# Two weight chunks ahead of each layer norm by token tiles, a weight rounding behind the norm, an offset from a tensor and a scalar

## The chip, the cores and the metric

The kernel runs on one core of one Trainium2 chip. The metric is the device time of one execution in microseconds (us); the median of three runs before the change is 1275.93 us (1275.86 to 1277.51).

## What is computed

Two blocks of two layers each on 256 tokens of width 1024, in fp32. The first block (attention of three kinds and squared-ReLU MLPs, RMS norms) isn't touched. In the second block each layer has a mixer and a gated feed-forward part, and after each of them a residual and a layer norm:

```python
for layer in range(DEPTH):                      # DEPTH = 2
    y = even_mixer(x, ...) if layer % 2 == 0 else odd_mixer(x, ...)
    x = layer_norm(ALPHA * x + y, ln1_g[layer], ln1_b[layer])
    f = conv_ffn(x, ffn_w_up[layer], ...)       # 1024 -> 2 x 2816, conv, silu(gate) * val, 2816 -> 1024
    x = layer_norm(ALPHA * x + f, ln2_g[layer], ln2_b[layer])

def layer_norm(x, g, b):
    mu = x.mean(-1, keepdims=True)
    var = jnp.square(x - mu).mean(-1, keepdims=True)
    return (x - mu) * lax.rsqrt(var + LN_EPS) * g + b
```

The kernel numbers these four layer norms 5 (after the even mixer), 6 (after the first feed-forward part), 7 (after the odd mixer) and 8 (the last one, whose result is the output).

## The kernel before, in words

**Weights as a stream.** All weights come as 186 chunks of 1 MB (128 partitions x 2048 fp32) in one fixed order. To keep fp32 precision, each chunk is split in two: ScalarE rounds it into `w_hi` (`cut`, L1090), GpSimd subtracts and rounds the rest into `w_lo` (L2350, four instructions of 512 columns a chunk). TensorE multiplies in three products (`three`, L284 to L286: hi by hi, hi by lo, lo by hi), or in two instructions in `dense_beside` (L332, L334). There are 3 buffers for the raw chunk and 4 for the split one. SyncE loads raw chunk c when `w_lo` of chunk c-3 is made. `cut(c)` waits for that load and for TensorE's last use of chunk c-4 (`chunk_used`), and TensorE waits for `w_lo_ready` of a chunk before it uses it.

**The order by hand.** No scheduler orders the work: each engine has its own program, written out line by line, and runs in order. ScalarE's `cut` of a chunk therefore stands at a fixed place between its other work, three chunks ahead (`AHEAD = 3`) of the step beside which it is written. `chunks_and_root` (L1101) issues the cuts that belong to the last chunks ahead of a norm and then loads the table of the square root.

**The work ahead of a norm.** There are two token tiles, t = 0 and t = 1, of 128 tokens each, and two output halves of 512 columns. Ahead of norms 5 and 7, `last_half` works through the last two chunks of the mixer's output projection (`ev_out`, `od_out`): chunk 2 with both token tiles side by side, step by step as its four inputs come in, then (for norm 7 after `sums`, which makes the root mean square of the gated heads) chunk 3, first all of t = 0, then all of t = 1. Ahead of norms 6 and 8, `down_by_tokens` works through 11 chunks with both token tiles side by side, except the last chunk, which is done for t = 0 first.

**The norm.** `norm` of VectorE has a `piece(n, t)` for each half and token tile: the residual is added (L1670, L1672 or L1674), statistics are taken (L1681), and with the second half the mean and variance (L1683). ScalarE makes the square root (L1175), VectorE's `invert(t)` the reciprocal (L1688) and the offset -mean x inverse (L1689, `scalar_tensor_tensor` on 128x1), and ScalarE normalises with them (L1188; L1182 in norm 8). VectorE works through its pieces in the order (0,0), (0,1), (1,0), then `invert(0)`, (1,1), `invert(1)`. TensorE turns the normalised tiles from tokens by features to features by tokens (`turned`, L401, 16 transposes), VectorE and ScalarE apply gain and bias and split the result into `xs_hi` and `xs_lo` (L1600), and TensorE goes on with the next stage: `fup0` after norm 5, `dt` and `od_xbc` after norm 6, `fup1` after norm 7. After norm 8 the result is stored in four transfers.

**Behind a norm.** ScalarE's first work behind norms 5 and 7 is the cut of fup chunk 3, then in `gated` one cut an iteration. Behind norm 6 it is the cut of `od_xbc` chunk 2, then Abs, Exp and Ln of the step sizes (L1507 to L1509), Exp (L1510), and per `od_xbc` chunk one cut, two activations (L1516) and a Silu (L1519), with VectorE's taps (L2253) in between.

Of the kernel before, what the change touches and what calls it, by code (L numbers as in the profile page):

```python
# [18 lines left out]
ALU = mybir.AluOpType  # L19
# [4 lines left out]
TT = T // P  # L24
# [9 lines left out]
AHEAD = 3  # L34
# [10 lines left out]
START, _n = {}, 0  # L45
# [27 lines left out]
def build(nc, x, stream, params, consts, onehot, logc, relb, evb_row, ln_rows, pool_w, pool_mat, vec_row, vec_scratch, out):  # L73
    with ExitStack() as ctx:
# [5 lines left out]
        def S(name):  # L80
            if name not in sems:
                sems[name] = ctx.enter_context(nc.semaphore(name))
            return sems[name]
# [27 lines left out]
        with hidden:  # L111
            hT_hi = hidden.enter_context(nc.sbuf_tensor("hT_hi", [P, 32, T], F32R))
            hT_lo = hidden.enter_context(nc.sbuf_tensor("hT_lo", [P, 32, T], F32R))
# [59 lines left out]
        sums = bank[7]  # L173
        r_bc, eps_s, r_col = rstd[:, :], mu[:, :], small[:, 60:62]

        deviation, inverse, offset, inv_y = (stats[:, 24 + 2 * n:26 + 2 * n] for n in range(4))
        moments = [stats[:, 32 + 2 * t:34 + 2 * t] for t in range(TT)]
# [34 lines left out]
        XS, n = {}, 0  # L212
# [5 lines left out]
        HT, n = {}, 0  # L218
# [10 lines left out]
        def claim(pe, key):  # L229

            while turn[0] % 8 >= rotating[0]:
                turn[0] += 1
            b = turn[0] % 8
            turn[0] += 1
            return claim_bank(pe, key, b)
# [11 lines left out]
        def filled(ins, key):  # L247
            b = made[key][0]
            fcount[b] += 1
            ins.then_inc(S(f"bank{b}_filled"), 1)  # L250
            made[key][2:] = [f"bank{b}_filled", fcount[b]]

        def filled_by_chunk(key, c):
            made[key][2:] = ["chunk_used", c + 1]
# [18 lines left out]
        def _(pe):  # L273
# [6 lines left out]
            def used_up(ins):  # L280
                ins.then_inc(S("chunk_used"), 1)
# [57 lines left out]
            def half_views(c):  # L339
                return (x.rearrange("p a b -> p (a b)").rearrange("p (k n) -> p k n", k=4) for x in chunk(c))  # L340
# [16 lines left out]
            def by_tokens(o, hi, lo, kw, src, k, t, start, stop):  # L357

                s = slice(t * P, (t + 1) * P)
                return three(o[:, :], src[0][:, k, s], src[1][:, k, s], hi[:, kw, :], lo[:, kw, :], start=start, stop=stop)  # L360

            def last_half(name, i, src, wait, sums=lambda: None):

                c = START[name] + 2
                hi, lo = half_views(c)
                o = [claim(pe, (name, 1, t)) for t in range(TT)]
                for k in range(4):
                    pe.wait_ge(S("xs_ready"), XS[wait] - 3 + k)
                    for t in range(TT):
                        last = by_tokens(o[t], hi, lo, k, src, k, t, start=(k == 0), stop=(k == 3))  # L370
                used_up(last)
                for t in range(TT):
                    filled_by_chunk((name, 1, t), c)
                sums()
                hi, lo = half_views(c + 1)
                for t in range(TT):
                    o = claim(pe, (name, 1, 2 + t))
                    for k in range(4):
                        last = by_tokens(o, hi, lo, k, src, k, t, start=(k == 0), stop=(k == 3))
                    if t == 0:  # L380
                        filled(last, (name, 1, 2))
                used_up(last)
                filled_by_chunk((name, 1, 3), c + 1)
                turned(i)
# [20 lines left out]
            def down_by_tokens(name, kt, ready, i):  # L405

                chunks, o = 2 * kt // 4, {}
                for c in range(chunks):
                    hi, lo = half_views(START[name] + c)
                    steps = [(u, t) for u in range(4) for t in range(TT)] if c < chunks - 1 else \  # L410
                        [(u, t) for t in range(TT) for u in range(4)]
                    for u, t in steps:
                        n, k = divmod(4 * c + u, kt)
                        key = (name, 2 * n + t)
                        if n == 0 and t == 0:
                            pe.wait_ge(S("hidden_ready"), ready + k + 1)
                        if k == 0:
                            o[n, t] = claim(pe, key)
                        last = by_tokens(o[n, t], hi, lo, u, (hT_hi, hT_lo), k, t, start=(k == 0), stop=(k == kt - 1))
                        if k == kt - 1 and (n, t) != (1, 1):  # L420
                            filled(last, key)
                    used_up(last)
                filled_by_chunk((name, 3), START[name] + chunks - 1)
                if i < 8:
                    turned(i)
# [86 lines left out]
            hi, lo = chunk(START["va"])  # L512
            o = claim(pe, "va")
            for t in range(TT):
                for k in range(8):
                    s = slice(t * P, (t + 1) * P)
                    last = three(o[:, t * P:(t + 1) * P], xs_hi[:, k, s], xs_lo[:, k, s], hi[:, k, 0:P], lo[:, k, 0:P],
                                 start=(k == 0), stop=(k == 7))
# [5 lines left out]
            o = claim(pe, "qa_sums")  # L524
            for t in range(TT):
                for n in range(4):
                    last = mm(o[:, 4 * n + t:4 * n + t + 3:2], sq[:, n, t * P:(t + 1) * P], cc("blk", 128)[:, 0:128:64],
                              start=True, stop=True)
# [544 lines left out]
        def _(act):  # L1073
# [26 lines left out]

            def chunks_and_root(name, total, first=0):  # L1101

                for c in range(first, total):
                    cut(START[name] + c + AHEAD)
                warm(ACT.Sqrt)

# [63 lines left out]
            def norm(i):  # L1170

                g, b, p0 = ln_par(i)
                for t in range(TT):
                    act.wait_ge(S("variance"), 2 * (i - 5) + t + 1)
                    af(deviation[:, t:t + 1], moments[t][:, 1:2], ACT.Sqrt, bias=pc("eps_ln")).then_inc(S("deviated"), 1)  # L1175
                    if i == 8 and t == 1:
                        return
                    act.wait_ge(S("inverted"), 2 * (i - 5) + t + 1)
                    factor = dict(bias=offset[:, t:t + 1], scale=inverse[:, t:t + 1])
                    if i == 8:  # L1180
                        key = last_piece(i, 0, t)
                        drained(af(token_half(0, t), by_tile(bank[made[key][0]][:, :]), ACT.Identity, **factor), key)  # L1182
                        continue
                    key = last_piece(i, 1, t)
                    o = bank[made[key][0]]
                    for n in PAIRS if t == 0 else (0, 1):
                        src = token_pair(n, t) if n < 2 else by_tile(o[:, (n - 2) * T:(n - 1) * T])
                        ins = af(token_pair(n, t), src, ACT.Identity, **factor)  # L1188
                        if n == 3:
                            drained(ins, key)  # L1190
                        else:
                            ins.then_inc(S("normed_act"), 1)

                def affine(n):
                    o = full(act, ("turn", i, n))
                    for j in range(2):
                        k = 2 * n + j
                        af(o[:, j * T:(j + 1) * T], o[:, j * T:(j + 1) * T], ACT.Identity, bias=pc(b, p0 + k),
                           scale=pc(g, p0 + k)).then_inc(S("affine_act"), 1)

                def high(n):
                    if n < 2:
                        act.wait_ge(S("affine_dve"), 2 * (i - 5) + n + 1)
                    else:
                        act.wait_ge(S("affine_act"), 4 * (i - 5) + 2 * n - 2)
                    o = bank[made[("turn", i, n)][0]]
                    af(xs_hi[:, 2 * n:2 * n + 2, :], o[:, :].rearrange("p (a b) -> p a b", a=2), ACT.Copy).then_inc(S("xs_hi"), 1)

                affine(2)
                high(0)  # L1210
                high(2)
                high(1)
                affine(3)
                high(3)

            def mlp(name, opened=False):
                hb = HT[name]
# [366 lines left out]
        def _(dve):  # L1584
# [75 lines left out]
            def norm(i, factor=None):  # L1660
# [24 lines left out]
                def invert(t):  # L1685

                    dve.wait_ge(S("deviated"), 2 * (i - 5) + t + 1)
                    link(v.reciprocal(inverse[:, t:t + 1], deviation[:, t:t + 1]))  # L1688
                    v.scalar_tensor_tensor(offset[:, t:t + 1], moments[t][:, 0:1], -1.0, inverse[:, t:t + 1], ALU.mult, ALU.mult)\  # L1689
                        .then_inc(S("inverted"), 1)  # L1690

                def gained(n, t):
# [8 lines left out]
                        .then_inc(S("result_dve"), 1)  # L1701

                piece(0, 0)
                piece(0, 1)
                piece(1, 0)
                if i == 8:
                    dve.wait_ge(S("ln_rows_loaded"), 16 * 4)
# [10 lines left out]
                    finished(0, 1)  # L1718
                    return
                invert(0)  # L1720
                piece(1, 1)
                invert(1)
                key = last_piece(i, 1, 1)
# [891 lines left out]
```

## Time and profile before

| | |
|---|---|
| median of three runs | 1275.93 us |
| the profiled execution, its own time | 1281.55 us |
| its span (first to last instruction) | 1279.7 us |
| TensorE busy | 1211.6 us (95%) |
| GpSimd busy | 955.8 us (75%) |
| ScalarE busy | 679.5 us (53%) |
| VectorE busy | 623.2 us (49%) |
| mean granted TensorE clock | 0.971 |

PE is TensorE, DVE is VectorE, ACT is ScalarE, POOL is GpSimd. A row of a timeline has the start in us from the span's start, the duration in us, the engine, the line, the operation, what it writes and reads, the shape, and in brackets the idle time just before it and who ended it. All instructions of the same kind that follow each other are merged into one row (x2, x4).

### The profile page before, as it was taken

What the parts mean: (1) busy time and instruction counts of PE and PEld (TensorE: products, weight loads), DVE (VectorE), ACT (ScalarE), POOL (GpSimd) and SP (SyncE); (2) the same over time, 40 slices, a digit from 0 to 9 for tenths busy, and PEclk for the clock granted to TensorE, in tenths of its full rate; (3) what the DMA queues carried; (4) which work ended last, traced back from release to release, by engine and by line L of the source; (5) the groups of instructions that cost most, each with busy time, mean ns of one, the idle gap of its engine ahead of it and who ended that gap; (6) DMA issues with size and microseconds to landing.
All of it is one profiled execution on the core that took longest, in us unless ns stands there. A gap on an engine that the chain in (4) does not pass through costs nothing.

```text
span 1279.7 us, 20261 instructions
## 1 busy us (share of the span) xinstructions
PE 1211.6 (95%) x7822; PEld 1081.0 (84%) x7822; DVE 623.2 (49%) x1076; ACT 679.5 (53%) x920; POOL 955.8 (75%) x750
## 2 busy tenths in 40 slices
PE   4899999999989999999999998999997898999997
PEld 4788998999968998999988777888886876888885
DVE  4866344210485244210542755777405646587712
ACT  5365655444565655444454346656546565656741
POOL 4846679978843779979795446899895854789985
PEclk9799999999999999999999898999998989999999
DMA  6562345554431446545553123555554442436551
GB/s 262 191 184 104 133 155 208 197 178 176 174 124 43 165 145 217 195 168 178 196 193 134 66 74 133 189 206 203 184 201 156 139 159 102 165 138 234 204 184 64
DMA packets 33132, 208.56 MB, mean 163 GB/s; under 512 B 3432, under 2 KB 7656, under 8 KB 8472
## 3 DMA queue, kind: packets, MB, share of 16 engines
q1 hardware_dynamic: 29728, 199.22, 43.6%
q10 hardware_dynamic: 3320, 8.14, 2.0%
q8 instruction: 62, 1.02, 0.3%
q14 instruction: 22, 0.18, 0.0%
HBM read 206.29 MB, written 1.59 MB: 162 GB/s over the span
## 4 chain that ended last, share of the span: by engine, by line
POOL 56%; issue 24%; PE 16%; DVE 2%; ACT 1%; DMA 0%; POOLq 0%; DVEq 0%; SPq 0%; ACTq 0%
POOL w_lo L2350 56%; PE bank L332 6%; PE bank L334 3%; PE bank L284 2%; PE bank L286 2%; PE bank L285 2%; ACT w_hi L1090 0%; DMA raw<-stream 0%; DVE stats L1681 0%; PE bank L1032 0%; ACT arena L1528 0%; ACT h L1188 0%; DVE bank L1695 0%; POOLq L2347 0%; PE bank L1047 0%
## 5 line engine op out<-in xcount | busy, mean ns | idle before, releaser
L2350 POOL TENSOR_TENSOR w_lo<-raw,w_hi 128x512 fp32r<-128x512 f32 x744 | 953.1, 1319 | 308.1 <-ACT w_hi L1090 307.9
L1090 ACT ACTIVATE w_hi<-raw 128x2048 fp32r<-128x2048 f32 x186 | 353.8, 1910 | 187.5 <-PE bank L286 110.0
L332 PE MATMUL bank<-xs,w_hi 128*128 128x512 f32 x1024 | 361.7, 398 | 3.1 <-DVE xs L1600 3.1
L334 PE MATMUL bank<-xs,w_lo 128*128 128x256 f32 x1024 | 287.3, 281 | 0.0
L332 PEld LDWEIGHTS bank<-xs,w_hi 128*128 128x128 f32 x1024 | 193.6, 189 | 50.4 <-issue 3.9
L284 PE MATMUL bank<-xs,w_hi 128*128 128x256 f32 x624 | 183.3, 294 | 20.6 <-POOL w_lo L2350 17.6
L284 PE MATMUL bank<-hT_hi,w_hi 128*128 128x256 f32 x680 | 194.7, 286 | 2.1 <-issue 1.9
L334 PEld LDWEIGHTS bank<-xs,w_lo 128*128 128x128 f32 x1024 | 194.5, 190 | 0.0
L286 PE MATMUL bank<-hT_hi,w_lo 128*128 128x256 f32 x680 | 192.4, 283 | 0.0
L285 PE MATMUL bank<-xs,w_hi 128*128 128x256 f32 x624 | 179.8, 288 | 0.0
L286 PE MATMUL bank<-xs,w_lo 128*128 128x256 f32 x624 | 179.4, 288 | 0.0
L284 PEld LDWEIGHTS bank<-xs,w_hi 128*128 128x128 f32 x624 | 122.8, 197 | 27.0 <-issue 26.2
L285 PE MATMUL bank<-hT_lo,w_hi 128*128 128x256 f32 x512 | 145.0, 283 | 0.0
L284 PEld LDWEIGHTS bank<-hT_hi,w_hi 128*128 128x128 f32 x680 | 128.6, 189 | 5.4 <-issue 5.2
L286 PEld LDWEIGHTS bank<-hT_hi,w_lo 128*128 128x128 f32 x680 | 128.6, 189 | 0.0
L285 PEld LDWEIGHTS bank<-xs,w_hi 128*128 128x128 f32 x624 | 123.0, 197 | 0.4 <-issue 0.2
L286 PEld LDWEIGHTS bank<-xs,w_lo 128*128 128x128 f32 x624 | 122.9, 197 | 0.0
L1762 DVE TENSOR_REDUCE tb<-bank 128x256 f32<-128x512 f32 x128 | 82.2, 684 | 63.9 <-PE bank L334 63.8
L1816 DVE SCALAR_TENSOR_TENSOR bank<-tb,par,bank 128x254 f32<-128x254 f32 (+1 forms) x176 | 85.8, 488 | 40.4 <-ACT bank L1253 35.7
L285 PEld LDWEIGHTS bank<-hT_lo,w_hi 128*128 128x128 f32 x512 | 96.6, 189 | 0.0
L284 PE MATMUL bank<-w_hi,hT_hi 128*128 128x512 f32 x212 | 84.3, 398 | 2.2 <-DVEq L2322 2.2
L285 PE MATMUL bank<-w_lo,hT_hi 128*128 128x512 f32 x212 | 83.7, 395 | 0.0
(318 smaller groups left out, 1600.5 us busy)
## 6 DMA issues: line engine op xcount, KB each, us to landing
raw<-stream SPq DMA_DIRECT2D x186, 1024.0 KB, 4.8
arena<-ln_rows ACTq DMA_DIRECT2D x4, 1024.0 KB, 4.9
arena<-vec_scratch ACTq DMA_DIRECT2D x8, 256.0 KB, 9.0
con<-consts SPq DMA_DIRECT2D x1, 1288.0 KB
h<-x SPq DMA_DIRECT2D x1, 1024.0 KB, 5.0
out<-h SPq DMA_DIRECT2D x4, 256.0 KB, 2.3
con<-pool_mat ACTq DMA_DIRECT2D x1, 768.0 KB, 8.1
vec_scratch<-vec_row ACTq DMA_DIRECT2D x1, 512.0 KB
```

The lines of the kernel that those rows point to most:

```text
L284: mm(out, lh, rh, start=start, stop=False, skip_group_check=True)
L285: mm(out, lh, rl, start=False, stop=False, skip_group_check=True)
L286: return mm(out, ll, rh, start=False, stop=stop, skip_group_check=True)
L332: mm(o[j][:, :], hi[:, k, s], xs[:, k, :, :].rearrange("p a t -> p (a t)"), start=(k == tiles_in[0]), stop=False, skip_group_check=True)
L334: last = mm(o[j][:, 0:T], lo[:, k, s], xs_hi[:, k, :], start=False, stop=(k == tiles_in[-1]), skip_group_check=True)
L1090: af(w_hi[:, c % CUT].rearrange("p a b -> p (a b)"), raw[:, c % RAW, :], ACT.Copy)\
L1762: ins = v.tensor_reduce(tb[:, i % 2, j * T:(j + 1) * T], o[:, :].rearrange("p (a t) -> p t a", a=2), AX.X, ALU.add)
L1816: ins = v.scalar_tensor_tensor(t[:, j, tap:T], u[:, j, 0:T - tap], pc("fcw", 132 * layer + 44 * (2 - tap) + ti), t[:, j, tap:T], ALU.mult, ...
L2350: ins = nc.gpsimd.tensor_tensor(w_lo[:, slot_c].rearrange("p a b -> p (a b)")[:, part], raw[:, slot_r, part], w_hi[:, slot_c].rearrange("p ...
```

## The change

It does four things. (1) `last_half` now ends chunk 2 of t = 0 first, goes through chunk 3 of t = 0, and then does what is left of chunk 2 and all of chunk 3 for t = 1. (2) `down_by_tokens` does its last two chunks, not the last one alone, for t = 0 first and then for t = 1. (3) The last cut ahead of norms 5, 6 and 7 (chunk 2 of `fup0`, chunk 1 of `od_xbc`, chunk 2 of `fup1`) moves behind ScalarE's part of the norm. (4) The offset is made by `tensor_scalar` from the mean, the inverse (a scalar for each partition) and -1.0; and in norms 5 and 7 `piece(0, 1)` moves behind `invert(0)`.

```diff
@@ last_half
-                for k in range(4):
-                    pe.wait_ge(S("xs_ready"), XS[wait] - 3 + k)
-                    for t in range(TT):
-                        last = by_tokens(o[t], hi, lo, k, src, k, t, start=(k == 0), stop=(k == 3))
-                used_up(last)
+                steps = [(0, 0), (0, 1), (1, 0), (1, 1), (2, 0), (3, 0)]
+                for k, t in steps:
+                    if t == 0:
+                        pe.wait_ge(S("xs_ready"), XS[wait] - 3 + k)
+                    last = by_tokens(o[t], hi, lo, k, src, k, t, start=(k == 0), stop=(k == 3))
+                filled(last, (name, 1, 0))
+                sums()
+                hi2, lo2 = half_views(c + 1)
                 for t in range(TT):
-                    filled_by_chunk((name, 1, t), c)
-                sums()
-                hi, lo = half_views(c + 1)
-                for t in range(TT):
-                    o = claim(pe, (name, 1, 2 + t))
+                    if t == 1:
+                        for k in (2, 3):
+                            last = by_tokens(o[1], hi, lo, k, src, k, 1, start=False, stop=(k == 3))
+                        used_up(last)
+                        filled_by_chunk((name, 1, 1), c)
+                    o2 = claim(pe, (name, 1, 2 + t))
                     for k in range(4):
-                        last = by_tokens(o, hi, lo, k, src, k, t, start=(k == 0), stop=(k == 3))
+                        last = by_tokens(o2, hi2, lo2, k, src, k, t, start=(k == 0), stop=(k == 3))
@@ down_by_tokens (step(c, hi, lo, u, t) is the body of the old inner loop)
+                for c in range(chunks - 2):
                     hi, lo = half_views(START[name] + c)
+                    for u in range(4):
+                        for t in range(TT):
+                            last = step(c, hi, lo, u, t)
                     used_up(last)
+                final = {c: tuple(half_views(START[name] + c)) for c in (chunks - 2, chunks - 1)}
+                for t in range(TT):
+                    for c in final:
+                        hi, lo = final[c]
+                        for u in range(4):
+                            last = step(c, hi, lo, u, t)
+                        if t == 1:
+                            used_up(last)
@@ chunks_and_root
-                for c in range(first, total):
+                for c in range(first, total - 1):
@@ norm of ScalarE, at its end
                 affine(3)
                 high(3)
+                cut(START[{5: "fup0", 6: "dt", 7: "fup1"}[i]] - 1 + AHEAD)
@@ invert of VectorE
-                    v.scalar_tensor_tensor(offset[:, t:t + 1], moments[t][:, 0:1], -1.0, inverse[:, t:t + 1], ALU.mult, ALU.mult)\
+                    v.tensor_scalar(offset[:, t:t + 1], moments[t][:, 0:1], inverse[:, t:t + 1], -1.0, ALU.mult, ALU.mult)\
                         .then_inc(S("inverted"), 1)
@@ norm of VectorE
                 piece(0, 0)
-                piece(0, 1)
+                if i in (6, 8):
+                    piece(0, 1)
                 piece(1, 0)
...
                 invert(0)
+                if i in (5, 7):
+                    piece(0, 1)
                 piece(1, 1)
                 invert(1)
```

## Rows read from the trace of the kernel before

**Rows 1.** The page: TensorE's busy time, and the chain that ended last, by engine.
```profile
PE 1211.6 (95%) x7822; PEld 1081.0 (84%) x7822; DVE 623.2 (49%) x1076; ACT 679.5 (53%) x920; POOL 955.8 (75%) x750
...
POOL 56%; issue 24%; PE 16%; DVE 2%; ACT 1%; DMA 0%; POOLq 0%; DVEq 0%; SPq 0%; ACTq 0%
```

**Rows 2.** Busy time by stretch: stretch, us, busy of each engine, clock, DMA share, GB/s.
```profile
775.70:783.00 7.30, 3.62 (x18) 2.40 (x17) 5.94 (x14) 5.67 (x13) 1.67 (x2) 0.76 0.46 177
783.00:786.40 3.40, 3.40 (x11) 2.92 (x12) 1.94 (x3) 2.51 (x5) 0.00 (x0) 0.51 0.00 0
...
968.10:979.40 11.30, 3.92 (x17) 2.77 (x17) 9.91 (x14) 5.66 (x13) 4.45 (x4) 0.70 0.52 186
...
1087.20:1090.10 2.90, 2.90 (x9) 2.51 (x10) 1.95 (x3) 2.05 (x5) 0.00 (x0) 0.50 0.02 6
```

**Rows 3.** Timeline of VectorE in norm 6.
```profile
965.47 0.70 DVE L1674 SCALAR_TENSOR_TENSOR bank<-h,bank 128x512 f32<-128x512 f32 x1 [25.08 <-PE bank L286]
...
968.00 4.57 DVE L1689 SCALAR_TENSOR_TENSOR stats<-stats 128x1 f32<-128x1 f32 x1
972.49 0.68 DVE L1674 SCALAR_TENSOR_TENSOR bank<-h,bank 128x512 f32<-128x512 f32 x1
```

**Rows 4.** Timeline of GpSimd around norm 6.
```profile
953.85 18.70 POOL L2350 TENSOR_TENSOR w_lo<-raw,w_hi 128x512 fp32r<-128x512 f32 x15
982.90 5.04 POOL L2350 TENSOR_TENSOR w_lo<-raw,w_hi 128x512 fp32r<-128x512 f32 x4 [10.35 <-ACT w_hi L1090]
```

**Rows 5.** Timeline of TensorE ahead of norm 5: 21 matmuls lie between the two starts.
```profile
770.57 0.39 PE L286 MATMUL bank<-w_hi,hT_hi 128*128 128x512 f32 x1
...
775.33 0.39 PE L286 MATMUL bank<-w_hi,hT_hi 128*128 128x512 f32 x1
```

**Rows 6.** Timeline of ScalarE behind norm 6.
```profile
980.92 1.91 ACT L1090 ACTIVATE w_hi<-raw 128x2048 fp32r<-128x2048 f32 x1
983.32 0.42 ACT L1507 ACTIVATE arena<-arena 8x256 f32<-8x256 f32 x1 [0.50 <-DVE arena L2239]
```

**Rows 7.** Timeline of VectorE in norm 5.
```profile
776.09 0.69 DVE L1672 TENSOR_TENSOR bank<-bank,h 128x512 f32<-128x512 f32 x1
...
778.42 0.16 DVE L1688 RECIPROCAL stats<-stats 128x1 f32<-128x1 f32 x1 [0.67 <-ACT stats L1175]
```

**Rows 8.** Timelines of VectorE in norm 7, and of TensorE's gated sums ahead of it.
```profile
1069.29 0.48 DVE L2302 SCALAR_TENSOR_TENSOR xs<-bank,par,xs 128x256 fp32r<-128x256 f32 x1 [0.56 <-ACT xs L1540]
...
1073.76 0.75 DVE L1670 SCALAR_TENSOR_TENSOR h<-bank,stats,h 128x512 f32<-128x512 f32 x1
...
1080.27 0.75 DVE L1670 SCALAR_TENSOR_TENSOR bank<-bank,stats,h 128x512 f32<-128x512 f32 x1
...
1082.61 0.17 DVE L1688 RECIPROCAL stats<-stats 128x1 f32<-128x1 f32 x1 [0.61 <-ACT stats L1175]
...
1071.31 1.84 PE L1063 MATMUL bank<-con,arena 128*128 128x1 f32 x16
```

**Rows 9.** Timelines of VectorE in norm 8, and of GpSimd's last roundings.
```profile
1268.30 0.70 DVE L1674 SCALAR_TENSOR_TENSOR bank<-h,bank 128x512 f32<-128x512 f32 x1 [25.06 <-PE bank L286]
...
1271.81 0.68 DVE L1674 SCALAR_TENSOR_TENSOR bank<-h,bank 128x512 f32<-128x512 f32 x1
...
1249.12 12.53 POOL L2350 TENSOR_TENSOR w_lo<-raw,w_hi 128x512 fp32r<-128x512 f32 x10
```

**Rows 10.** Behind norm 5: TensorE's line L332 (22 chunks), GpSimd's next rounding, VectorE's first fold.
```profile
L332 PE MATMUL bank<-xs,w_hi x352: 391/395/764, 783.0 to 907.7; 128*128 128x512 f32 x176
...
787.46 5.05 POOL L2350 TENSOR_TENSOR w_lo<-raw,w_hi 128x512 fp32r<-128x512 f32 x4 [10.08 <-ACT w_hi L1090]
...
790.36 1.29 DVE L1762 TENSOR_REDUCE tb<-bank 128x256 f32<-128x512 f32 x2 [5.03 <-PE bank L334]
```

**Rows 11.** Other VectorE instructions with operands in SBUF: line L2061, line L2242.
```profile
L2061 DVE TENSOR_SCALAR arena<-arena,par x1: 1425/1425/1425, 623.4 to 623.4; 12x256 f32<-12x256 f32 x1
...
L2242 DVE SCALAR_TENSOR_TENSOR arena<-arena x1: 831/831/831, 987.4 to 987.4; 8x256 f32<-8x256 f32 x1
```

More of the change, by code:

```diff
@@ L407, in down_by_tokens, with step @@
                 chunks, o = 2 * kt // 4, {}
-                for c in range(chunks):
-                    hi, lo = half_views(START[name] + c)
[L410 to L421, printed above, removed]
-                    used_up(last)
+                def step(c, hi, lo, u, t):
+                    n, k = divmod(4 * c + u, kt)
+                    key = (name, 2 * n + t)
+                    if n == 0 and t == 0:
+                        pe.wait_ge(S("hidden_ready"), ready + k + 1)
+                    if k == 0:
+                        o[n, t] = claim(pe, key)
+                    last = by_tokens(o[n, t], hi, lo, u, (hT_hi, hT_lo), k, t, start=(k == 0), stop=(k == kt - 1))
+                    if k == kt - 1 and (n, t) != (1, 1):
+                        filled(last, key)
+                    return last
+                for c in range(chunks - 2):
+                    hi, lo = half_views(START[name] + c)
+                    for u in range(4):
+                        for t in range(TT):
+                            last = step(c, hi, lo, u, t)
+                    used_up(last)
+                final = {c: tuple(half_views(START[name] + c)) for c in (chunks - 2, chunks - 1)}
[6 more added lines that the diff above has]
+                            used_up(last)
                 filled_by_chunk((name, 3), START[name] + chunks - 1)
```

## The prediction

> **What bounds the kernel.** I began with the page: TensorE is busy 95% of the span, yet most of the chain that ended last is GpSimd's rounding [rows 1]. A chunk costs GpSimd some 5.05 us and TensorE 5.67 us (22 chunks in the 124.7 us between the first and last start of L332) [rows 10]. So in a dense stage TensorE sets the pace and the rounding follows closely: moving a rounding costs nothing only while a stock of finished chunks lasts. The stretches at the norms then show where TensorE stands: 7.3 us in norm 5 and 11.3 us in norm 6, with under 4 us of work in each [rows 2]. There the chain is VectorE, ScalarE, transposes, VectorE. In VectorE's timeline of norm 6 one row stands out: the offset, a single column, takes 4.57 us [rows 3]. It ends when GpSimd's continuous run ends, 953.85 + 18.70 = 972.55 [rows 4]. Piece (1,1), whose matmuls had long ended (968.1), starts only after it, at 972.49.
>
> **A first look at the pace.** One fp32 matmul of 512 columns takes (775.33 - 770.57) / 21 = 0.227 us [rows 5]; a unit of three 0.68, one token tile of a chunk (12) 2.72, a whole chunk 5.44 us. The change neither adds nor removes a matmul.
>
> **Norm 6.** Token tile 0 now ends one half chunk earlier: its last piece starts at 965.47 - 2.72 = 962.75 [rows 3]. Up to the offset it takes 968.00 - 965.47 = 2.53 us, so the offset is issued at 965.3. GpSimd still rounds the chunk before until some 967.7 (972.55 less one chunk of 5.0) [rows 4]. The price of the new instruction has bounds: 0.16 us if it doesn't need what GpSimd holds, or a wait to 967.7, 2.4 us, if it does. `tensor_scalar` with both sides in SBUF has taken 1.43 us where GpSimd ran [rows 11], so I take the wait. It costs nothing here: TensorE is busy with tile 1 until 968.1, and ScalarE's four normalisations (some 0.5 us each, 2.0) end at 969.7, when the variance of tile 1 is due (968.15 + 1.65, the 2.53 less root and reciprocal, = 969.8). The cover is TensorE's own work on tile 1. Piece (1,1) starts at 968.15 instead of 972.49: 4.34 us. The root of tile 1 no longer queues behind those normalisations; the same wait in norm 5 was 0.67 us, and 0.36 without a queue: another 0.3. TensorE would restart at 979.4 - 4.65 = 974.75.
>
> That isn't yet the gain, since the moved cut now stands on ScalarE's queue. ScalarE's part of the norm ended at 980.92; now at 976.3. Then come two cuts of 1.91 us, to 980.1, and then Abs, which had started at 983.32 [rows 6]. The earlier limit, the end of `dt` and one VectorE step of 0.5 us, lies at 978.6 and isn't last any more. So what follows moves by 3.2 us, not 4.65. In `od_xbc` the loop of cut, activations and taps on ScalarE and VectorE is slower than TensorE and sets the pace, so 3.2 us is what goes on. The chunk whose rounding moved is ready at 978.2 + 5.05 = 983.3; TensorE needs it after `dt` (3.4 us) and `od_xbc` chunk 0 (48 matmuls of 0.12, 5.8 us), at 974.75 + 9.2 = 983.9 at the earliest. It is close, but TensorE doesn't set the pace there. **-3.2 us** (bounds -2.2, if TensorE restarts at half rate for all of `dt`, and -4.65).
>
> **Norm 5.** Chunk 2 of tile 0 ends two units (1.36 us) earlier. VectorE then takes (0,0), waits for tile 0's second half (30 units of 0.227 after 764.9: 771.7), inverts at 773.7 to 774.1, and does (0,1) until 775.5. TensorE ends at 775.7, so (1,1) starts at 775.8 instead of 776.09: 0.3 us; the root without a queue gives 0.3 [rows 7]. Here TensorE restarts at half rate: 0.51 granted (1.2 GHz) from 783.0 to 786.4, behind a norm in which it mostly stood [rows 2]. If full rate comes back at the same moment, only half of a start 0.6 us earlier remains: **-0.3 us** (bounds 0 and -0.6).
>
> The moved cut costs nothing as long as the stock holds. The first cut behind the norm started 1.9 us ahead of its rounding at 787.46 [rows 10]; 0.6 us earlier the moved one takes its place, 784.9 to 786.8, its rounding until 791.8, the next one until 796.9. TensorE needs them at 790.36 + 5.6 = 796.0 and 801.6 [rows 10], some 4 us later each, and GpSimd gains 0.6 us a chunk. In ScalarE's queue both cuts end at 788.7, ahead of the first fold at 790.36 that it waits for. The raw loads behind it, three chunks on, land 6 us before their cuts. Norm 7's stock is alike.
>
> **Norm 7.** The last input is ready at 1069.77. Ahead of the sums TensorE then has one unit left instead of two, and these start at 1070.5 instead of 1071.31: 0.8 us [rows 8]. But TensorE, which used to fill the wait for that input with tile 1, stands about 0.7 us, and ends at 1079.2 instead of 1078.6. VectorE: (0,0) at 1072.9, (1,0) at 1075.0 when its bank is full, offset by 1077.5, (0,1) until 1079.0, (1,1) at 1079.25 instead of 1080.27 [rows 8]: 1.0 us, and 0.25 for the root (0.61 against 0.36). Half rate again (0.50) from 1087.2 to 1090.1 [rows 2]: **-0.6 us** (bounds -0.3 and -1.3).
>
> **Norm 8.** Tile 0's chain moves from 1268.30 to 1265.6 and is out of the way; (1,1) starts when TensorE ends, 1270.97, instead of 1271.81 [rows 9]. The rest is unchanged: **-0.8 us**.
>
> **Edits without a price.** The offset as `tensor_scalar` changes nothing by itself once no rounding runs beside it (norms 5, 7, 8) or it is hidden (6). Semaphores, transfers and bytes stay as they are; SyncE's load for the moved chunk has landed long before.
>
> **Sum.** -0.3 - 3.2 - 0.6 - 0.8 = -4.9 us, against the profiled execution: 1281.55 to 1276.6. That execution lies 5.6 us above the median of the runs; taken from the median, 1275.93 - 4.9 = 1271.0.
>
> **A rule against the trace.** The offset outlasted four GpSimd instructions of some 1.25 us [rows 3, 4]. The Trainium skill (SBUF — State Buffer, "Who interferes with whom") says that whoever issues first gets the shared port pair "for the whole instruction", and the other blocks; by that alone one waits for one instruction, at most 1.3 us, and norm 6 would have had 3.3 us less to give. The row shows more than three times that. The same section says that `tensor_scalar` can enter a mode that takes the pair too; L2061 agrees.
>
> **Rivals.**
> *A. The 4.57 us belong to the profiled execution.* The 5.6 us between it and the median are suspiciously like it. If the offset gets through at the first end of a GpSimd instruction (968.9), piece (1,1) started at 969.0 in the timed runs, norm 6 gives 1.1 us at the restart, and the second cut takes that back at Abs (980.1 against 979.8). What remains is -0.3 - 0.6 - 0.8 + 0.3 = -1.4: **1274.5**. For it: in most rows like L2242 the wait is under 1.3 us. Against it: the program is the same in each run, and GpSimd ran without a pause. 0.22.
> *B. A half-rate stretch of TensorE more or less.* Such a stretch costs about 1.7 us (half of 3.4) [rows 2]. One less: -6.6, **1269.3**, 0.12; it would show in the clock of the restarts.
> *C. A lockout behind norm 6.* After the change GpSimd rounds three chunks back to back there, 978.3 to 993.4. L2242, with both inputs in SBUF, is issued at 984.2; it took 0.83 us where GpSimd's chunk had just ended [rows 11]. If it is held as the offset was, until GpSimd pauses at 993.4, the taps start at 994.8 instead of 988.4, and `od_xbc` is 6.4 us late: -4.9 + 6.4 = +1.5, **1277.4**. It decides once the wait passes the 2.2 us that VectorE has there. With A it would be about 1281. 0.07.
> *D. The change doesn't get tile 0 earlier,* because TensorE waits for `w_lo` of the last chunk, which it now needs 2.72 us sooner. At norm 8 the rounding ends at 1261.65 [rows 9] and is needed at 1262.8 (1268.2 less two token tiles of a chunk), so only if GpSimd slips by over 1.1 us; norms 6 and 8 then give half, 2.0 us less: **1273.0**, 0.04.
>
> **Numbers.** The forecast, 1271.0, has 0.55. Its bounds, -3.3 and -7.3, give 1268.6 to 1272.6; A asks for 1274.5 and some tenths, so 1268.3 to 1275.2 leaves out C and the tails. About 0.2% (2.6 us) can be told from no change: faster is the forecast, B and most of D, 0.73; same is A and most of C, 0.22; slower 0.05.
>
> **What would show it.** The offset of norm 6's tile 1 at 0.16 us; piece (1,1) within 0.1 us of TensorE's last matmul in all four norms; TensorE's stretch without main matmuls in norm 6 near 6.7 us instead of 11.3; two cuts back to back behind each of norms 5 to 7, and Abs right behind them; no wait for `w_lo` in fup chunks 2 to 5. I am wrong if Abs moves by the full 4.6 us, if L2242 takes over 2 us, or if the profile gains 5 us and the timed runs don't.

## The result, and the profile after

The changed kernel took 1269.65 us (median of 5 runs, 1267.99 to 1270.86) against 1275.93 for the one before (5 runs): ratio 0.9947, interval 0.9921 to 0.9972, so 6.3 us less. The forecast was 1271.0 us. The profiled execution took 1269.36 us with a span (first to last instruction) of 1267.6, 12.1 us under the span of before. That is more than the timed gain, so the first question is where the two traces part. One execution of the kernel before in the last group below took 4124.69 us; it is in no comparison.

The page of the changed kernel; beside it belong [rows 1]:
```profile
PE 1205.4 (95%) x7822; PEld 1076.6 (85%) x7822; DVE 609.6 (48%) x1076; ACT 679.1 (54%) x920; POOL 957.2 (76%) x750
...
POOL 71%; issue 27%; PE 1%; POOLq 0%; DVE 0%; DVEq 0%
```
Every engine has as many instructions as before. The largest difference is VectorE's: it is busy 13.6 us less (623.2 to 609.6), and 12.4 us of that was waiting inside two instructions, shown below; TensorE is busy 6.2 us less.

To place the time I cut every trace where TensorE gives a weight chunk free. There are 186 such releases, in the same order in all kernels. A norm's stretch is the last two chunks ahead of it and what follows until the first chunk behind it is released (for norm 6 that chunk is `dt`). "mixer" lies between the stretches of norms 6 and 7; "end" is the last two chunks and all behind them; "start" is what comes before norm 5's stretch. "sum" is the three norms and the end, "+ mixer" the same with the mixer, and the last columns are the last two chunks ahead of norms 6 and 8 alone. From the semaphore updates in the traces, in us:
```
kernel           start   norm5  norm6  mixer  norm7  end    sum     + mixer  6 / 8
before           764.85  25.49  25.57  80.92  30.63  19.71  101.40  182.32   10.88 / 10.88
before_again     753.88  25.48  25.58  81.00  30.69  19.70  101.45  182.45   10.88 / 10.88
after            755.12  25.29  22.46  81.15  30.01  19.69   97.45  178.62   11.67 / 11.66
after_again      753.25  25.12  23.56  81.09  30.02  19.73   98.43  179.51   12.86 / 11.71
offset_only      754.15  24.79  22.67  81.87  27.83  19.81   95.10  176.96   10.88 / 10.88
cut_only         765.29  24.65  22.07  81.71  29.38  19.71   95.81  177.53   10.88 / 10.88
offset_and_cut   756.13  24.79  22.14  81.47  29.42  19.81   96.16  177.63   10.88 / 10.88
tokens_only      753.21  28.68  25.28  81.43  32.99  19.21  106.16  187.61   11.69 / 11.25
after_stt        754.61  24.96  23.48  81.32  32.34  19.26  100.04  181.36   12.86 / 11.29
lazy             764.80  25.14  22.64  80.48  32.24  18.90   98.92  179.40   10.88 / 10.88
down_tiles       753.16  24.82  22.04  81.19  29.48  18.90   95.24  176.43   10.88 / 10.88
before_norope    761.12  25.10  28.72  80.36  32.08  19.71  105.61  185.97   10.88 / 10.88
after_norope     761.47  24.97  24.64  80.43  32.26  19.31  101.18  181.60   12.89 / 11.29
```
Of the 12.1 us, 9.7 lie in the start, in code that the change does not touch; 3.95 lie in the norms and the end; the other stages took about 1.5 us longer (the stretch of `fup1` alone 1.2).

Windows of the changed kernel at the norms, columns as in [rows 2]:
```profile
766.00:772.60 6.60, 2.44 (x17) 1.71 (x16) 5.73 (x13) 4.55 (x11) 0.00 (x0) 0.84 0.06 24
773.00:777.30 4.30, 4.30 (x15) 3.72 (x14) 1.37 (x2) 4.27 (x4) 1.50 (x2) 0.50 0.00 0
959.00:965.30 6.30, 2.03 (x17) 1.51 (x15) 5.51 (x13) 3.84 (x9) 0.00 (x0) 0.98 0.42 164
...
1073.00:1077.60 4.60, 4.57 (x14) 3.92 (x15) 1.99 (x3) 4.57 (x6) 1.13 (x1) 0.50 0.01 4
```
Norm 6 is the third line: 6.3 us where [rows 2] had 11.3, and GpSimd is not busy in it at all (0.00; 4.45 before). Behind norms 5 and 7 TensorE still restarts at a granted clock of 0.50.

Behind norm 6 the restart is different from before. `dt`, before and now:
```profile
979.40:982.80 3.40, 3.38 (x26) 3.18 (x27) 1.96 (x3) 3.37 (x5) 0.00 (x0) 1.00 0.00 0
```
```profile
965.30:969.80 4.50, 4.50 (x26) 4.50 (x27) 1.93 (x3) 4.47 (x6) 1.08 (x1) 0.65 0.00 0
```
The same matmuls took 4.5 us at a granted clock of 0.65 where they had taken 3.4 at 1.00: 1.1 us of the earlier restart was lost again at once. before_again took 3.4 us as well; in all other profiles below `dt` took 4.4 to 5.5.

VectorE's timeline in norm 6:
```profile
955.67 0.17 DVE L1706 RECIPROCAL stats<-stats 128x1 f32<-128x1 f32 x1 [0.36 <-ACT stats L1192]
955.87 0.21 DVE L1707 TENSOR_SCALAR stats<-stats 128x1 f32<-128x1 f32 x1
959.01 0.70 DVE L1692 SCALAR_TENSOR_TENSOR bank<-h,bank 128x512 f32<-128x512 f32 x1 [2.93 <-PE bank L286]
...
961.05 0.17 DVE L1706 RECIPROCAL stats<-stats 128x1 f32<-128x1 f32 x1 [0.36 <-ACT stats L1192]
961.25 0.21 DVE L1707 TENSOR_SCALAR stats<-stats 128x1 f32<-128x1 f32 x1
...
974.39 0.91 DVE L2263 SCALAR_TENSOR_TENSOR arena<-arena 8x256 f32<-8x256 f32 x1 [3.84 <-ACT arena L1527]
```
The 4.57 us of [rows 3] are gone. Piece (1,1), at 959.01, now waits for TensorE; in all four norms it starts within 0.1 us of the end of TensorE's last chunk. The last line (L2242 in the kernel before) is rival C's candidate: 0.91 us.

GpSimd's timeline around norm 6:
```profile
938.91 18.78 POOL L2371 TENSOR_TENSOR w_lo<-raw,w_hi 128x512 fp32r<-128x512 f32 x15
968.72 21.80 POOL L2371 TENSOR_TENSOR w_lo<-raw,w_hi 128x512 fp32r<-128x512 f32 x16 [11.03 <-ACT w_hi L1107]
```
The first run lasts until 957.69, so tile 0's offset (955.87) was issued beside it and still took 0.21 us.

ScalarE's timeline behind norm 6:
```profile
966.74 3.71 ACT L1107 ACTIVATE w_hi<-raw 128x2048 fp32r<-128x2048 f32 x2
970.34 0.40 ACT L1525 ACTIVATE arena<-arena 8x256 f32<-8x256 f32 x1
```
Two cuts back to back and Abs right behind, as forecast. `dt` ends at 969.78, so the other limit, `dt` and one VectorE step of 0.5 us, lies at the same place.

TensorE's waits between 947 and 953 us:
```profile
PE bank L284 <- POOL w_lo L2371: 0.5, 1, 0.5
```
This one was not forecast. It lies ahead of norm 6, and there is one like it ahead of norm 8: the last two chunks took 10.88 us before and 11.67 and 11.66 now.

### The profile page after: what moved, and what is told of

It reads as the page before. It is cut to its first block, busy times and chain, and to the rows that moved or that the text cites. A ratio compares the mean times of both kernels' runs of the same rounds, so it can differ in the third digit from the quotient of the medians.

```text
span 1267.6 us, 20263 instructions
## 1 busy us (share of the span) xinstructions
PE 1205.4 (95%) x7822; PEld 1076.6 (85%) x7822; DVE 609.6 (48%) x1076; ACT 679.1 (54%) x920; POOL 957.2 (76%) x750
## 4 chain that ended last, share of the span: by engine, by line
POOL 71%; issue 27%; PE 1%; POOLq 0%; DVE 0%; DVEq 0%
POOL w_lo L2371 71%; PE bank L284 0%; PE bank L286 0%; PE bank L285 0%; POOLq L2368 0%; DVE bank L1713 0%; POOLq L2377 0%; DVE stats L1699 0%; DVE bank L1692 0%; DVEq L74 0%; DVE h L1718 0%; DVE stats L1701 0%; DVE stats L1707 0%; POOLq L2371 0%; DVE stats L1706 0%
## 5 line engine op out<-in xcount | busy, mean ns | idle before, releaser
L332 PE MATMUL bank<-xs,w_hi 128*128 128x512 f32 x1024 | 364.3, 401 | 3.9 <-DVE xs L1618 3.8
L332 PEld LDWEIGHTS bank<-xs,w_hi 128*128 128x128 f32 x1024 | 194.4, 190 | 52.4 <-issue 4.4
```

The source lines that it names most:

```text
L332: mm(o[j][:, :], hi[:, k, s], xs[:, k, :, :].rearrange("p a t -> p (a t)"), start=(k == tiles_in[0]), stop=False, skip_group_check=True)
```

## The experiments

Kernels of one group ran on the same chip and share the runs of the kernel before: first the repeats and the pair without one multiplication; then the single parts with after_stt; then lazy, offset_and_cut and down_tiles. The medians of the kernel before in the three groups are 1274.56, 1275.99 and 1275.17 us, and each ratio is against its own group.

**Both kernels again, unchanged.** Edit: none.

> The kernel before, once more, against itself. Theory 1 (lockouts by chance): the profile of before lost 9.1 us in one VectorE multiplication in the first 50 us (two SBUF inputs, held while GpSimd rounded two chunks), which the profile of after did not (1.04 us there), in code that the change doesn't touch. Then the profile of this run may show any length from 0.7 to 9 us for it, while the offset of norm 6 may be 4.6 us or less; the timed runs lie between 1272 and 1278. Rival: the lockouts are the same in each execution of one program; then this profile shows 9.1 us and 4.57 us again, within 0.1 us.

> The changed kernel, once more. Theory 1: ratio 0.995 +- 0.003, and the early multiplication (L1880) may be long here too in some executions (single times near 1277 would show it). Rival: it is 1.04 us again, and all times are within 1268 to 1271.

Measured: before_again 1274.51 us, ratio 1.0007 (0.9991 to 1.0022); after_again 1269.98, ratio 0.9967 (0.9954 to 0.9981), 4.6 us under the 1274.56 of before on that chip. The runs of before_again fall into two bands, six at 1271.6 to 1272.8 and six at 1276.2 to 1278.6. None of after_again is near 1277; they lie between 1266.8 and 1273.4.

VectorE's line of the offset in before_again (duration min/median/max in ns):
```profile
L1689 DVE SCALAR_TENSOR_TENSOR stats<-stats x8: 159/160/4747, 764.6 to 1265.7; 128x1 f32<-128x1 f32 x8
```
The norm 6 wait came again, 4.75 us: it does not belong to one execution, and rival A falls. In norms 5 and 7 the other long ones took 0.61 and 1.26. But before_again's start was 11.0 us shorter than before's. VectorE and GpSimd at the first rope pass, in the kernel before:
```profile
39.14 9.10 DVE L1859 TENSOR_TENSOR arena<-arena 128x512 f32<-128x512 f32 x1
...
29.03 18.66 POOL L2350 TENSOR_TENSOR w_lo<-raw,w_hi 128x512 fp32r<-128x512 f32 x15
```
And in the changed kernel:
```profile
39.46 1.04 DVE L1880 TENSOR_TENSOR arena<-arena 128x512 f32<-128x512 f32 x1
...
29.92 29.24 POOL L2371 TENSOR_TENSOR w_lo<-raw,w_hi 128x512 fp32r<-128x512 f32 x22
```
The same instruction, untouched by the change, took 9.10 us once and 1.04 once, with GpSimd rounding beside it both times (0.78 in before_again, 0.79 in after_again). This is most of what the two profiles differ by beyond the norms, and no part of the gain. It is not tied to the old kernel: the profiled executions of cut_only and lazy had it too and took 1279.25 and 1281.44 us, 11 and 12 above their medians. A median of 6 to 12 runs may hold any share of such executions, so read the stretches beside the ratios.

**The multiplication that was held, left out of both kernels.**
```diff
-                link(v.tensor_tensor(pair_of(n), pair_of(n), over(c, 2), ALU.mult))
```

> The kernel before without the multiplication of the queries and keys by the cosine in VectorE's rotation of the first block (L1859, left out in all three calls; its output is another). Theory 1: what is gained is the mean lockout, some 3 to 6 us: 1270 to 1273. If the timed runs don't have the lockout: 1 to 2 us for the instructions themselves, 1274 to 1275.

> The changed kernel with the same multiplication left out. Against the kernel before with it left out, this is the change alone: by the profiles -0.2 (norm 5), -3.1 (norm 6), -0.6 (norm 7), -0.75 (end), +0.8 (TensorE waits 0.5 us twice for w_lo of the last chunk ahead of norms 6 and 8, since both chunks are waited for at the start), and 0 or +1.2 for TensorE's pitch in fup1: -2.7 to -3.9. If the timed 6.3 us belong to the change, it is 1263 to 1267 and the difference stays over 5.

Measured: 1283.07 us, ratio 1.0068 (1.0046 to 1.0089), and 1278.33, ratio 1.0026 (1.0012 to 1.0040). Both got slower with less to do, against the expectation. VectorE's next instruction with two inputs in SBUF, in before_norope:
```profile
L1873 DVE TENSOR_TENSOR arena<-arena x1: 12570/12570/12570, 45.6 to 45.6; 128x512 f32<-128x512 f32 x1
```
In after_norope the same one took 12.53. The wait moved to the next candidate and grew by a third, so as a way to remove it the experiment failed. As a comparison it serves: with the wait alike in both, the pair differs by 4.7 us in the medians (2.7 to 3.9 had been expected, and over 5 if all of the first 6.3 were the change's) and by 4.4 in the stretches. The old offset of norm 6 was held again, 5.04 us.

**The offset alone, in the kernel before.**
```diff
-  v.scalar_tensor_tensor(offset[:, t:t + 1], moments[t][:, 0:1], -1.0, inverse[:, t:t + 1], ALU.mult, ALU.mult)
+  v.tensor_scalar(offset[:, t:t + 1], moments[t][:, 0:1], inverse[:, t:t + 1], -1.0, ALU.mult, ALU.mult)
```

> The kernel before with the offset by tensor_scalar alone. In the profile of after that instruction took 0.21 us while GpSimd rounded. Theory 1 (it doesn't take what GpSimd holds; the lockout of the offset is most of what norm 6 gave): 0.2 us for all eight, VectorE's piece (1,1) of norm 6 starts at once when TensorE ends, 4.3 us earlier, and since one cut alone stands ahead of Abs, 3.5 to 4.6 us of it go on; in norm 7 the 1.26 us become 0.2, worth 0.5 to 1: together -4 to -5.5 us, as much as the whole change. Rival (it is held too where a rounding runs all the time, and 0.21 us was luck): the offset of norm 6 takes 2 to 5 us, and the time is that of before within 1 us.

Measured: 1268.57 us, ratio 0.9954 (0.9925 to 0.9983). Timelines of VectorE and GpSimd in norm 6:
```profile
956.10 0.21 DVE L1689 TENSOR_SCALAR stats<-stats 128x1 f32<-128x1 f32 x1
...
949.97 11.18 POOL L2350 TENSOR_TENSOR w_lo<-raw,w_hi 128x512 fp32r<-128x512 f32 x9
```
In the middle of GpSimd's run the new form takes 0.21 us, as do all eight. This edit alone removes the wait, and with it 6.3 us of the norms' stretches (101.4 to 95.1), 5.4 with the mixer; 4 to 5.5 had been expected. The excess is norm 7's, 2.8 us less where 0.5 to 1 had been expected: in this execution TensorE restarted there at a clock of 1.00 (see rival B). The runs scatter widely, six at 1265.4 to 1267.1 and three at 1277.7 to 1279.2.

**The three cuts alone, in the kernel before.**
```diff
-                for c in range(first, total):
+                for c in range(first, total - 1):
...
+                cut(START[{5: "fup0", 6: "dt", 7: "fup1"}[i]] - 1 + AHEAD)
```

> The kernel before with the three cuts moved behind the norms alone; the offset is the old form. Theory 1: GpSimd has nothing to round when the offset of norm 6 is issued (its last rounding ends 0.3 us before), so 0.16 us; TensorE restarts 4.6 us earlier, but two cuts stand ahead of Abs, so 3.1 us go on; with norm 7's 0.5 to 1 us: -3 to -4. It should be worth about 1.4 us less than the offset alone. Rival: if the cuts in front of Abs cost nothing, it equals the offset alone, and fup stays as it is in both.

Measured: 1268.15 us, ratio 0.9928 (0.9911 to 0.9946). VectorE in norm 6, and GpSimd:
```profile
967.36 0.16 DVE L1690 SCALAR_TENSOR_TENSOR stats<-stats 128x1 f32<-128x1 f32 x1
967.77 0.70 DVE L1675 SCALAR_TENSOR_TENSOR bank<-h,bank 128x512 f32<-128x512 f32 x1 [0.26 <-PE bank L286]
...
959.74 7.50 POOL L2351 TENSOR_TENSOR w_lo<-raw,w_hi 128x512 fp32r<-128x512 f32 x6
```
The old form takes 0.16 us; GpSimd ended at 967.24, 0.12 us ahead of it, a narrow margin seen in one profile. So this edit too removes the wait by itself: 5.6 us of the stretches, 4.8 with the mixer, where 3 to 4 had been expected. Its profiled execution had the early wait again (8.85 us, start 765.29).

**The token tiles alone.** The diff of TensorE's functions and VectorE's piece order as ahead of the prediction; offset and cuts as before.

> The kernel before with the order by token tiles (and VectorE's piece order) alone. Theory 1: nothing is gained. The cut ahead of each norm now waits for TensorE's later last use of its buffer (2.7 us later), and the table load and the root of tile 0 stand behind it on ScalarE: in norm 5 and 7 +1 to +2 us; in norm 6 the old offset is issued while GpSimd still rounds two chunks and is held to their end: 0 to +1; at the end -0.7, and +0.5 to +2 for TensorE's wait for w_lo of the last chunk in each of the two down parts: +1 to +4 in all. Rival (the order by tiles is where the gain is): -2 to -4.

Measured: 1277.85 us, ratio 1.0020 (1.0007 to 1.0034). ScalarE at norm 5:
```profile
761.45 1.92 ACT L1107 ACTIVATE w_hi<-raw 128x2048 fp32r<-128x2048 f32 x1 [6.24 <-PE bank L286]
763.39 1.28 ACT L1116 ACT_TABLE_LOAD   x1
764.79 0.28 ACT L1192 ACTIVATE stats<-stats,par 128x1 f32<-128x1 f32 x1
```
The cut ahead of the norm waits for the chunk that TensorE now releases last, and the table load and root stand behind it. The stretches grow by 4.7 us, the median by 1.9. So the order by tiles is not where the gain is. In the whole change the moved cut clears that queue (norm 5 is back from 28.68 to 25.29), so cuts and tiles belong together. The old offset of norm 6 was not held to the end of GpSimd's run here, as had been expected; it took 0.65 us, and GpSimd rounded on for 2.4 us.

**The change with the old offset.** Edit: the offset's diff, reversed, in the changed kernel.

> The changed kernel with the old form of the offset. Theory 1: no difference from the changed kernel beyond 0.3 us, since no rounding runs beside seven of the eight offsets, and in norm 6 tile 0's is held at most until the rounding ahead ends, under TensorE's work on tile 1. Rival: the offset is held and tile 0's transposes are late: +2 to +4 against the changed kernel.

Measured: 1269.92 us, ratio 0.9942 (0.9925 to 0.9958), as the whole change. The old form waited once, in norm 6, for 1.83 us, which lay under TensorE's work on tile 1. Beside cuts and tiles the new offset is worth nothing measurable in the times. The stretches are 1.6 to 2.6 us longer than those of the changed kernel, through norm 7 (32.34), which the next experiment takes up; no offset was held there.

**Late waits.** In the changed kernel, TensorE waits for the last chunk where it first needs it, no longer ahead of both.
```diff
-                final = {c: tuple(half_views(START[name] + c)) for c in (chunks - 2, chunks - 1)}
+                final = {}
                 for t in range(TT):
-                    for c in final:
+                    for c in (chunks - 2, chunks - 1):
+                        if t == 0:
+                            final[c] = tuple(half_views(START[name] + c))
```

> The changed kernel, but the split chunks of the last two in the down part are waited for one at a time: the last one when TensorE comes to it, 2.7 us later than in the change. Theory 1: the two last chunks take 10.9 us again instead of 11.7 to 12.9 ahead of norm 6 and 11.3 to 11.7 ahead of norm 8, and both stretches end that much earlier: -1.5 to -2.5 us against the changed kernel in the sum over the norms. Rival (the rounding itself is too late for the order by tiles): the wait moves to the last chunk, and nothing is gained.

Measured: 1269.45 us, ratio 0.9960 (0.9934 to 0.9985). The last two chunks are back at 10.88 us ahead of norms 6 and 8, and the end went from 19.69 to 18.90: the 0.8 us forecast for norm 8. Norm 6 gained nothing over after (22.64 against 22.46), because `dt` now ran at half clock (1.2 GHz) throughout, 5.5 us. Norm 7 got longer, 30.01 to 32.24, so the 1.5 to 2.5 us expected did not come. Window of lazy ahead of norm 7:
```profile
1069.80:1073.20 3.40, 3.40 (x10) 2.62 (x9) 1.61 (x3) 0.17 (x2) 1.24 (x2) 0.50 0.25 46
```
A stretch at half clock now lies ahead of the norm, in the matmuls of the last two chunks; in after these ran at 1.00. after_stt shows the same (32.34), and so does after_norope (32.26), whose code from norm 5 on is the changed kernel's own. So neither the late waits nor the old offset is needed for it: three of five executions with the new order ahead of norm 7, the cut moved, have it. What decides whether it comes is not shown.

**Offset and cuts, without token tiles; then with tiles in the down part alone.** down_tiles is lazy with the mixers' last half and VectorE's piece order put back as before.

> The kernel before with the offset by tensor_scalar and the three cuts moved, no order by token tiles anywhere. Theory 1: either of the two takes the lockout away, so together they are worth what one is: the four norm stretches sum to 95 to 96 us, as with the cuts alone (95.8), against 97.5 to 98.4 in the changed kernel and 101.4 before. Rival (the order by tiles carries a part that these two can't): 98 or more.

> Offset and cuts as in the change, the order by token tiles only in the down part (norms 6 and 8) with the late wait, and the mixers' last half as before. Theory 1: the best of all: norm 5 and 7 as with the cuts alone (24.7 and 29.4), norm 6 at 21.3 to 21.9 and the end at 18.9 (0.8 us less than before, as forecast): 94.3 to 94.9, some 1 us less than without any order by tiles, and faster than the changed kernel by 2 to 3 us. Rival: the order by tiles gives nothing even so, 95.8.

Measured: offset_and_cut 1268.22 us, ratio 0.9941 (0.9915 to 0.9967); down_tiles 1266.61, ratio 0.9927 (0.9901 to 0.9954). VectorE's last piece in down_tiles:
```profile
1257.02 0.70 DVE L1690 SCALAR_TENSOR_TENSOR bank<-h,bank 128x512 f32<-128x512 f32 x1 [1.72 <-PE bank L286]
```
The piece waits for TensorE, and TensorE waits for no `w_lo` there. Its median is the lowest of all: 8.6 us under its own 1275.17 of before, and 3 us under the change. The intervals of the three kernels of this group overlap, so its place ahead of offset_and_cut is seen in the medians and the end's stretch (18.90 against 19.81), not proved by the ratio. The stretches, 96.2 and 95.2, are near the 95 to 96 and the 94.3 to 94.9 expected. offset_and_cut lacks only the order by tiles, and its stretches are 1.3 and 2.3 us shorter than in the two profiles of the changed kernel (97.5 and 98.4): as the change has it, that order costs time.

## Why the prediction was right, and where not

The direction was right, and so was the main mechanism, the wait inside norm 6's offset. The timed gain is near the forecast 4.9 us: 6.3 at first, 4.6 repeated, 4.7 in the pair without the multiplication. The traces place only 3.0 to 4.0 of it in the norms and the end, so a part of the agreement is luck. The terms compare so (trace of after, then after_again, against before):

- **Norm 6, -3.2.** It was forecast for Abs. Abs starts 26.1 us behind the beginning of norm 6's stretch in before, 23.0 and 24.2 in the two profiles of after: -3.1 and -1.9. Offset 0.21 us, piece (1,1) when TensorE ends, and Abs behind two cuts came as told. Two things on the way did not. TensorE's wait for `w_lo` ahead of the norm, put at nothing, is 0.8 and 2.0 us. And `dt` was taken to run as fast as before (3.4 us, with half rate as a bound): it took 4.5 and 4.4. Against them, piece (1,1) to TensorE's restart got shorter than forecast: it came 4.2 and 3.1 us earlier, 5.0 in both without the wait, where 4.65 was forecast.
- **"I take the wait"** for the new form beside GpSimd was wrong: 0.21 us in after and in offset_only. L2061, a `tensor_scalar` of 256 columns [rows 11], was the wrong neighbour. The 2.4 us would have been hidden, so the sum did not suffer; but it hid that either edit alone would do.
- **Norm 5, -0.3.** Measured -0.2 and -0.4, but not for the reason given. The forecast took it from the order by tiles; cut_only and offset_only, without that order, have -0.8 and -0.7.
- **Norm 7, -0.6.** Measured -0.6 both times. It is loose: it ran from 27.83 to 32.99 us over the kernels, by what is at half clock and, in tokens_only, by the queue on ScalarE. Here too cut_only has more without the order by tiles, -1.2.
- **Norm 8, -0.8.** Measured 0.0. This step failed. The tail did get 0.8 shorter (8.83 to 8.03), but the last two chunks got 0.8 longer. I let TensorE need the last chunk one token tile of a chunk (2.72 us) sooner; the code takes the views of both chunks, and waits for both, in one line ahead of both, so it is needed a full chunk sooner, 5.44 us. The wait of rival D was there, at another place than named: not because GpSimd slips, but because TensorE asks too soon. lazy shows it, by getting the 0.8 back.
- **Sum.** In the traces -3.95 and -3.0 (against before_again -4.0 and -3.0), under the 4.9 forecast by norm 8 and the waits. The timed difference is larger, 4.6 on the same chip. I can't place the remainder of 0.6 to 1.6 us in the change, and the single parts have one too: offset_only and cut_only lie 7.4 and 7.8 us under their group's median, with 5.4 and 4.8 in the traces. Between the profiled executions of before_again and after_again the spans differ by 4.7: 3.0 in the norms and the end, 1.2 in the stretch of `fup0` and 0.6 in the start, both in code that is alike.
- **Slips.** GpSimd's chunk before ends at 972.55 - 5.0 = 967.55, not 967.7; nothing hangs on it. The chances of the forecast, B and D add up to 0.71, so the 0.73 for faster is too high.

**Rivals.** A is false: 4.57, 4.75 and 5.04 us in three profiles of kernels with norm 6 as before. Its argument, that 5.6 us between profile and median look like those 4.57, pointed at something real in the wrong place: the profile's excess was a wait in the start. Only the reason given against it, that the program is the same in each run, was weak: for L1859 the same program gave 0.8 and 9.1. B did not come in the changed kernel: the clock behind norms 5 and 7 is 0.50 as before, and behind norm 6 it is lower than before (0.65, was 1.00), which is the other way round. That its 1269.3 lies nearer to the measured 1269.65 than the forecast does is chance. But the price it names is real. The windows of offset_only and of cut_only behind norm 7:
```profile
1071.30:1076.00 4.70, 4.70 (x27) 4.17 (x28) 1.89 (x3) 3.38 (x4) 0.40 (x1) 1.00 0.02 3
```
```profile
1083.00:1087.40 4.40, 4.40 (x19) 3.78 (x18) 1.59 (x3) 4.37 (x5) 1.32 (x2) 0.61 0.02 4
```
A clock of 1.00 against 0.61: the norm up to the first chunk behind it took 12.80 us in the one and 14.36 in the other, so a half-rate stretch less was worth 1.6 us here (1.7 in the forecast).

C is false: 0.91, and GpSimd was rounding. D came in another form, as told.

**The rule.** By the Trainium skill (SBUF — State Buffer, "Who interferes with whom"), whoever issues first has the shared port pair for the whole instruction, and the other is blocked. Mostly the traces agree, with a wait of one GpSimd instruction, at most 1.3 us. Over all 13 profiles I counted VectorE's two-tensor instructions without a PSUM tile that began while GpSimd was rounding: 753. In 735 at most one GpSimd instruction ended before they did, in ten two; the other eight outlasted 4 to 10, and each ended within 0.6 us of the end of GpSimd's run. Three of the eight are norm 6's offset, in three of three executions with the old order and the old cut.

**What stays open.** What decides between the short and the long wait. It is neither the run's length (1.04 us inside a run of 29.24 us) nor simply the moment within the GpSimd instruction: held ones began 0.14 to 1.13 us into it, others through the whole length. Nor is it the form alone: of 13 old offsets that began beside GpSimd nine took 0.60 to 1.27 us, one 1.83 and three 4.57 to 5.04. Nor do the bands of before_again follow: the profile with the 9.10 us took 1281.55, above both, and before_again's, without the early wait, took 1271.90, in the lower band; none of the upper band was profiled.

## What to carry to other kernels

Look for a tiny VectorE instruction whose duration is many times that of its like; when it has two tensors in SBUF and GpSimd runs back to back beside it, change its form or move GpSimd's work, and expect the gain once: here either edit alone took the wait away (5.4 and 4.8 us with the mixer), and the two together gave no more (4.7). When an order of tiles is changed, look where the wait for each input stands in the code, not only when the input is first read, and what on other queues waits for the release that has moved. When an engine restarts earlier, look at its clock there too: here 1.1 us were lost again in `dt`. And take a profile twice before reading a difference from it: here 9.7 of 12.1 us lay in code that nobody had touched.

## What the runs showed of the hardware that was not expected

- An instruction with two SBUF inputs can be held 8.85 to 12.57 us in the start, or hardly (0.70 to 1.86): three of eleven executions showed the long wait on the rope's multiplication, and both without that multiplication on the next such instruction.
- A one-column `tensor_scalar` was not held beside GpSimd in any of nine cases (0.21 us, as without it). A one-column `scalar_tensor_tensor` was in all 13: 0.60 to 5.04 us, against 0.16 without.
- TensorE showed two steady paces at a granted clock of 1.00, 5.55 and 5.65 us for a chunk of `fup0` or `fup1`. `fup1` in the kernel before, and in before_again:
```profile
1094.30:1211.00 116.70, 116.55 (x336) 62.81 (x335) 1.00 0.54 196
```
```profile
1083.50:1201.40 117.90, 117.71 (x336) 62.88 (x335) 1.00 0.55 197
```
Equal work, 1.2 us apart. Over all kernels the 21 chunks behind the first took 116.7 to 116.8, 117.9 or 118.7 us: all at the faster pace, the first ten at the faster and the rest at the slower, or all at the slower. The kernel before had the first and the second of these for the same `fup1`. A difference of 2 us between two single profiles can be this alone.
